# Four dense feed-forward blocks by one level of Strassen's method, gate and up rounds ahead of the down rounds

## The reference, cut to what matters

```python
def _swiglu(h, w_gate, w_up, w_down):
    return (jax.nn.silu(h @ w_gate) * (h @ w_up)) @ w_down
```

## Time and profile before

| | us |
|---|---|
| median of 3 runs | 3219.03 |
| lowest, highest run | 3212.87, 3219.28 |
| span of the profiled execution | 3210.8 |
| PE busy in it | 3114.5 (97%) |
| DVE, ACT busy in it | 798.5 (25%), 487.2 (15%) |
| mean DMA rate over it | 197 GB/s |

### The profile page before, as it was taken

One profiled execution on the slowest core, in us unless ns is written; L12 is line 12 of the kernel. 1 busy time (PEld: TensorE's weight loads), 2 busy tenths in 40 slices (PEclk: granted clock), 3 DMA queues, 4 the chain that ended last, 5 costly groups with the idle time before them and its releaser, 6 DMA issues.

```text
span 3210.8 us, 40563 instructions
## 1 busy us (share of the span) xinstructions
PE 3114.5 (97%) x17087; PEld 2209.2 (69%) x17087; DVE 798.5 (25%) x1696; ACT 487.2 (15%) x1124; POOL 109.5 (3%) x122
## 2 busy tenths in 40 slices
PE   7999998999999999999998999998999999999998
PEld 3566666477777777677776677786777667767765
DVE  2566666410100233300355300132000000100101
ACT  2423332010000123200221200121000000000001
POOL 1121121000000000000000000000000000000000
PEclk8999999999999999999998999999999999999999
DMA  7333127254444522344310345433999999999997
GB/s 249 112 113 124 48 77 292 104 195 155 157 155 147 166 74 81 105 156 147 124 55 16 106 157 166 135 79 125 381 379 382 345 379 382 330 378 382 332 377 259
DMA packets 417831, 636.36 MB, mean 198 GB/s; under 512 B 11247, under 2 KB 304726, under 8 KB 410366
## 3 DMA queue, kind: packets, MB, share of 16 engines
q1 hardware_dynamic: 412317, 612.49, 55.4%
q0 software_dynamic: 5344, 21.46, 2.0%
HBM read 632.70 MB, written 1.20 MB: 197 GB/s over the span
## 4 chain that ended last, share of the span: by engine, by line
PE 89%; DVE 3%; SPq 2%; DMA 1%; ACT 1%; issue 1%; DVEq 1%; PEld 1%; PEldq 0%; ACTq 0%
PE PS L930 18%; PE PS L3830 11%; PE PS L938 7%; PE PS L1399 7%; PE PS L3851 6%; PE PS L3837 6%; PE PS L3877 3%; PE PS L705 2%; PE PS L1975 2%; PE PS L996 2%; PE PS L3324 2%; PE PS L1971 1%; PE PS L1549 1%; PE PS L288 1%; PE PS L1564 1%
## 5 line engine op out<-in xcount | busy, mean ns | idle before, releaser
L957 DVE TENSOR_TENSOR scratch<-scratch,PS 128x128 f32<-128x128 f32 (+1 forms) x182 | 61.7, 339 | 1278.8 <-ACT scratch L947 1278.4
L930 PE MATMUL PS<-XT,WO 128*128 128x256 f32 x1344 | 296.2, 379 | 0.1
L930 PE MATMUL PS<-XT,WF 128*128 128x256 f32 x1344 | 294.7, 379 | 0.0
L930 PEld LDWEIGHTS PS<-XT,WO 128*128 128x128 f32 x1344 | 255.2, 190 | 50.5 <-issue 17.7
L930 PEld LDWEIGHTS PS<-XT,WF 128*128 128x128 f32 x1344 | 255.3, 190 | 46.2 <-issue 12.9
L947 ACT ACTIVATE scratch<-PS 128x128 f32<-128x128 f32 (+1 forms) x200 | 64.9, 324 | 1413.9 <-PE PS L930 776.5
L1399 PE MATMUL PS<-XT,WH 128*128 128x512 f32 x512 | 240.9, 596 | 1.7 <-ACT XT L480 1.7
L3830 PEld LDWEIGHTS PS<-scratch,WO 128*128 128x128 f32 x1792 | 208.6, 192 | 24.9 <-issue 24.6
L3830 PEld LDWEIGHTS PS<-scratch,WF 128*128 128x128 f32 x1792 | 202.4, 192 | 21.3 <-issue 17.9
L3830 PE MATMUL PS<-scratch,WO 128*128 128x128 f32 x1792 | 209.1, 275 | 0.0
L3830 PE MATMUL PS<-scratch,WF 128*128 128x128 f32 x1792 | 207.2, 276 | 1.2 <-ACT scratch L3988 1.2
(11 more groups left out here) (578 smaller groups left out, 3782.6 us busy)
## 6 DMA issues: line engine op xcount, KB each, us to landing
XT<-in_moe_wg SPq DMA_DIRECT2D x56, 1024.0 KB, 10.9
scratch<-in_moe_wu SPq DMA_DIRECT2D x56, 1024.0 KB, 14.1
OT<-in_moe_wd SPq DMA_DIRECT2D x56, 1024.0 KB, 14.1
WO<-in_ada_w SPq DMA_DIRECT2D x36, 1024.0 KB, 7.2
WF<-in_moe_wg SPq DMA_DIRECT2D x28, 1024.0 KB, 15.2
WF<-in_moe_wu SPq DMA_DIRECT2D x28, 1024.0 KB, 17.1
WF<-in_moe_wd SPq DMA_DIRECT2D x28, 1024.0 KB, 12.0
WO<-in_moe_wg SPq DMA_DIRECT2D x28, 1024.0 KB, 11.2
```

What stands on the lines that cost most here:

```text
L930: mm = nc.tensor.matmul(k.PS[:, 4 + f, w * n:(w + 1) * n], slot.gu[:, w, kb, f * P:(f + 1) * P], rhs(kb), start=kb == 0, stop=kb == KB - 1)
```

## The change

Each product of a dense block is cut into 2 x 2 blocks and made from seven block products in place of eight. For a gate and up round the blocks are two tiles of 128 tokens (`t`), two halves of the features (`kh`) and two chunks of 128 hidden units (`fh`); a block product has 8 matmuls of 128 moving columns (gate and up, 4 feature chunks). For a down round they are two token tiles, two hidden chunks and two halves of the 1024 columns; a block product is one matmul of 512 columns. Four of the seven need differences of weight blocks, four need sums of token (or hidden) blocks, which DVE makes ahead; for round 0 of blocks 2 and 3 POOL makes the weight terms. Afterwards DVE puts the seven products together: in every gate and up round (`up_sums_vector`), but only once for the down rounds, since each of their seven products adds up over all rounds in a bank of its own.

All gate and up rounds of a block come first; the hidden units of all rounds stay in SBUF (`hall`); then come all down rounds. At the end, products 7 and 4 of the last 3 rounds (blocks 0, 1) or 6 rounds (blocks 2, 3) are put last (`KEPT`), so that the first token tile is complete earlier. The loops are written out. Raw gate and up weights go to WF and to a piece of scratch, their terms to OT and WO.

```diff
@@ tensor @@
+def up_product(k, m, r, i):
+    weights, tokens = up_sides(k, m, r, i)
+    out = up_place(k, m, r, i)
+    for w in range(2):
+        for kb in range(4):
+            mm = k.nc.tensor.matmul(out[:, w, :], weights[:, w, kb, :], tokens[:, kb, :], start=kb == 0, stop=kb == 3)
+    return mm
+
+def up_first_tensor(k, pe, m, r):
+    pe.wait_ge(*up_landed(k, m, r))
+    up_product(k, m, r, 1)
+    up_product(k, m, r, 2).then_inc(*k.up_pe[r % 2].done("a"))
+
+def up_rest_tensor(k, pe, m, r):
+    S = k.up_pe[r % 2]
+    pe.wait_ge(*terms_at(k, m, r))
+    for i in (4, 6):
+        up_product(k, m, r, i)
+    up_product(k, m, r, 7).then_inc(*S.done("d"))
+    up_product(k, m, r, 5).then_inc(*S.done("e"))
+
+def up_tensor(k, pe, m, r):
+    pe.wait_ge(*sum_at(k, m, r - 2, "sum"))
+    up_first_tensor(k, pe, m, r)
+    up_product(k, m, r, 3).then_inc(*k.up_pe[r % 2].done("raw"))
+    up_rest_tensor(k, pe, m, r)
...
+def ffn_tensor(k, pe, m, flip=None):
...
+    for r in range(2, UP_ROUNDS):
+        up_tensor(k, pe, m, r)
...
+    defer = UP_ROUNDS - KEPT[m]
+    pe.wait_ge(*sum_at(k, m, LAST_UP - 1, "sum"))
+    for q in range(3):
+        down_first_tensor(k, pe, m, q)
+    pe.wait_ge(*sum_at(k, m, LAST_UP, "sum"))
+    for q in range(3):
+        down_next_tensor(k, pe, m, q, (6, 5, 3, 7, 4)).then_inc(*k.dnt_pe.done("t"))
...
+    for q in range(3, UP_ROUNDS):
+        mm = down_first_tensor(k, pe, m, q)
...
+    for i in (7, 4):
+        for q in range(defer, UP_ROUNDS):
+            mm = down_product(k, m, q, i)
+        mm.then_inc(*k.fe_pe.done(f"p{i}"))
@@ vector @@
+def weight_terms(eng, t, block):
+    tt = eng.tensor_tensor
+    tt(t[0], block(0, 1), block(0, 0), ALU.subtract)
+    tt(t[2], block(1, 1), block(0, 1), ALU.subtract)
+    eng.drain()
+    tt(t[1], block(1, 1), t[0], ALU.subtract)
+    eng.drain()
+    return tt(t[3], t[1], block(1, 0), ALU.subtract)
...
+def up_sums_vector(k, dve, m, r):
...
+    dve.wait_ge(*up_copied(k, m, r, "p1"))
+    tt(c(0, 0), k.fp1, place(2), ALU.add)
+    dve.wait_ge(*up_at(k, m, r, "d"))
+    tt(k.fu2, k.fp1, place(6), ALU.add)
+    dve.drain()
+    tt(k.fu3, k.fu2, place(7), ALU.add)
+    dve.drain()
+    tt(c(1, 0), k.fu3, place(4), ALU.subtract)
+    dve.wait_ge(*up_at(k, m, r, "e"))
+    tt(c(0, 1), k.fu2, place(5), ALU.add)
+    tt(c(1, 1), k.fu3, place(5), ALU.add)
+    dve.drain()
+    tt(c(0, 1), c(0, 1), place(3), ALU.add).then_inc(*k.sum_dve[r % 2].done("sum"))
...
+def ffn_vector(k, dve, m, between={}, late=None):
+    for r in range(UP_ROUNDS):
+        up_sums_vector(k, dve, m, r)
+        if r + 2 < UP_ROUNDS:
+            up_terms_vector(k, dve, m, r + 2)
+        else:
+            down_terms_vector(k, dve, m, r + 2 - UP_ROUNDS)
+        hidden_vector(k, dve, m, r)
+        if r in between:
+            between[r]()
+    for q in range(2):
+        hidden_sums_vector(k, dve, m, q)
+    for q in range(2, UP_ROUNDS):
+        down_terms_vector(k, dve, m, q)
+        hidden_sums_vector(k, dve, m, q)
@@ sync @@
+def up_load(k, sp, m, r, weights, *free):
...
+    if r >= 2:
+        sp.wait_ge(*up_at(k, m, r - 2, "raw"))
+        sp.wait_ge(*terms_at(k, m, r - 2))
...
+def down_load(k, sp, m, q, weights, *free):
...
+    if q >= 3:
+        sp.wait_ge(*k.dnr_pe.at("raw", LAST_UP * m + q - 3))
@@ tensor_program @@
-    ffn_tensor(k, pe, 0, 2, lambda: flipped(0, 1, False, k.lno_dve.at("out", 9)), 2)
+    ffn_tensor(k, pe, 2, lambda: flipped(0, 1, False, k.lno_dve.at("out", 9)))
     flipped(1, 0, True, k.dg_dve.at("d", 0))
...
-    ffn_tensor(k, pe, 0, 3, lambda: flipped(2, 1, True, k.dg_dve.at("d", 3)), 1)
+    ffn_tensor(k, pe, 3, lambda: flipped(2, 1, True, k.dg_dve.at("d", 3)))
```

More of the change, by code:

```diff
@@ L138, in done, with __init__, at, both @@
         return self.sem, 1
+class Renamed:
+    def __init__(self, steps, names, past=0):
+        self.steps, self.names, self.past = steps, dict(zip(names.split(), steps.names, strict=True)), past
+    def at(self, name, rnd=0):
+        return self.steps.at(self.names[name], self.past + rnd)
+    def done(self, name):
+        return self.steps.done(self.names[name])
+    def both(self, first, second):
+        return self.steps.both(self.names[first], self.names[second])
 class Kern:
@@ new lines, in down_landed, with ffn_sync @@
+def down_landed(k, m, q):
+    return k.down_in[q % 2], 16 * (half_count(m, q) + 1)
+def ffn_sync(k, sp, m, weights, downs):
+    for r in range(2, LAST_UP - 1):
+        up_load(k, sp, m, r, weights)
+    for q in range(2):
+        before = [k.dnr_pe.at("raw", LAST_UP * (m - 1) + 9), k.fe_pe.at("p3", m - 1)][q:q + 1] if m == 1 else downs
+        down_load(k, sp, m, q, weights, *before)
+    for r in range(LAST_UP - 1, UP_ROUNDS):
+        up_load(k, sp, m, r, weights)
+    down_load(k, sp, m, 2, weights, up_at(k, m, LAST_UP - 1, "e"))
+    for q in range(3, UP_ROUNDS):
+        down_load(k, sp, m, q, weights)
@@ new lines, in down_bank, with down_first_tensor, down_next_tensor @@
+def down_bank(m, i):
+    return DOWN_BANKS[i] ^ (4 * FIRST_SET[m])
+def down_first_tensor(k, pe, m, q):
+    pe.wait_ge(*down_landed(k, m, q))
+    pe.wait_ge(*sum_at(k, m, q, "h"))
+    down_product(k, m, q, 1)
+    return down_product(k, m, q, 2)
+def down_next_tensor(k, pe, m, q, order):
+    pe.wait_ge(*k.dn_dve.at("s", up_count(m, q)))
+    for i in order:
+        mm = down_product(k, m, q, i)
+        if i == 3 and q < LAST_UP:
+            mm.then_inc(*k.dnr_pe.done("raw"))
+        elif i in (5, 6, 3) and q == LAST_UP:
+            mm.then_inc(*k.fe_pe.done(f"p{i}"))
+    return mm
@@ L1098, in end_by_tile_vector @@
[L1098 to L1108 removed]
+    act.wait_ge(*k.fe_pe.at("p12", m))
@@ new lines, in first_tile_vector @@
+def first_tile_vector(k, dve, m):
+    tt, bank = k.nc.vector.tensor_tensor, lambda i: k.PS[:, down_bank(m, i), :]
+    left, right = view(k, 0, 512), view(k, 512, 512)
+    dve.wait_ge(*k.fe_act.at("p1", m))
+    dve.wait_ge(*k.fe_pe.at("p6", m))
+    tt(k.du2, left, bank(6), ALU.add)
+    tt(left, left, bank(2), ALU.add)
+    dve.drain()
+    dve.wait_ge(*k.fe_pe.at("p5", m))
+    tt(right, k.du2, bank(5), ALU.add)
+    dve.drain()
+    dve.wait_ge(*k.fe_pe.at("p3", m))
+    tt(right, right, bank(3), ALU.add).then_inc(*k.lne_dve.done("evac0"))
@@ new lines, in second_tile_vector @@
+def second_tile_vector(k, dve, m, begin=True, end=True):
+    tt, bank = k.nc.vector.tensor_tensor, lambda i: k.PS[:, down_bank(m, i), :]
+    left, right = view(k, D, 512), view(k, D + 512, 512)
+    if begin:
+        dve.wait_ge(*k.fe_pe.at("p7", m))
+        tt(left, k.du2, bank(7), ALU.add)
+        dve.drain()
+        tt(right, left, bank(5), ALU.add)
+    if end:
+        dve.wait_ge(*k.fe_pe.at("p4", m))
+        tt(left, left, bank(4), ALU.subtract).then_inc(*k.lne_dve.done("evac1"))
```

541 lines of the change are left out of this document (323 added, 218 removed).

## The result

The changed kernel takes 3128.5 us (median; 3127.0 to 3129.7), the kernel before 3218.1: a ratio of 0.972, with an interval from 0.971 to 0.974. It saves 89.6 us. Forecast were 3124 us and a saving of 94.7.

The account below looks back on a forecast made before the run. PE was taken to bound the kernel in the four dense blocks. Gains of 104.0 us less losses of 9.3 gave 94.7, so 3219.0 - 94.7 = 3124 us, with a range of 3110 to 3135 (chance 0.70).

Parts of the forecast that it names:

- Gate and up on PE: In the dense blocks a gate and up round of 112 records takes 12.50 us, 1.32 less than before.
- The rival of a slower stream: Gate and up records of 128 columns run slower than the 111.6 ns taken: 3132 to 3149 us; chance 0.07.
- weight loads that show: Loads of 190 to 192 ns do not hide behind 128 columns: 396 us lost, 3520 us; chance 0.02.
- Down on PE: A down round has 14 records in place of 16: 6.01 us, 0.86 less.
- DVE: DVE's work is 9.0 of PE's 12.5 us in gate and up rounds, 4.2 of 6.0 in down rounds; cost 0.
- Its rival: DVE becomes the bound: whole gain gone at 14.7 us a round, about 3366 us at 18; chance 0.03.
- The step: From up to down in each block PE waits 1.2 us for DVE, four times: 4.8 us lost.
- Loads: Gate and up weights land 7.8 us after issue; cost 0, with 2.9 us of slack in the tightest place.
- Clearing and transposes: Bank clearing goes, 1.0 us a block with what surrounds it; transposes of blocks 0 and 1 save 2.6.
- Starts and ends: Starts lose 0 in blocks 0 and 1, 1.6 us in 3; ends lose 0.9, 1.3, 0.7 in 1, 2, 3.
- The first rival: The seams cost some 5 us more in each block: 3144 us, between 3135 and 3160; chance 0.14.
- I take that as unchanged: The runs' median stays 8.2 us above the profiled span after the change, as before it.

Follow-up runs that it names:

- dve4: The changed kernel with four more operations of 1024 elements on DVE ahead of each round's weight terms: 3220.1 us, 91.6 more.
- seam: The changed kernel, with DVE making the last hidden product and down round 0's sums before round 1's weight terms: 3122.2 us, 6.3 less.
- starts: The changed kernel, in blocks 2 and 3 with tile 1's transposes between PE's first products of rounds 0 and 1: 3124.3 us, 4.2 less.
- plain_both: The changed kernel's order of phases with eight plain block products everywhere, no terms or sums: 3216.7 us, ratio 1.0001 to the kernel before.
- after_again: The changed kernel unchanged, measured and profiled once more: 3127.5 us.

## Why the prediction was right, step by step

**The bound.** Right. PE ends the chain before and after, and records taken away were time saved: 52.6 and 61.8 us for the gate and up products (with Strassen's down rounds and with plain ones), 26.4 and 35.6 for the down products. Within the four blocks, without what differs elsewhere, it is 52.4 and 57.3, and 32.3 and 37.1.

**Gate and up on PE.** 12.50 us a round forecast, 12.51 measured; 16 records in 1.79 us are 112 ns each in the rounds behind a block's start. The rival of a slower stream is out, and so is that of weight loads that show. The ratio of 0.62 that the Trainium skill gives for 128 against 512 columns (TensorE: Matmul & The Clock Gate, Back-to-back issue gap) does not hold in this stream; in the changed kernel it is 112 to 429 ns, 0.26 again.

**Down on PE.** 6.01 forecast and found; the last rounds at 4.3 on PE ran without a wait, so the 5 us kept as an upper bound were not needed.

**DVE.** Forecast 9.0 of 12.5 us, busy for 8.2. Its rival was put at 14.7 us a round for the loss of the whole gain; at 13.66 (dve4) the gain was already gone. The sum behind that number counted only the steady rounds. It left out the rounds that also hold the end of a norm, and the slow records that follow a long wait. The conclusion for this kernel stood, but the margin was not one number: DVE's own work is 13.66 less four operations of 1.3, some 8.5 us, which leaves 4 us in a plain round and only 0.4 in a round with a norm's end of 3.6.

**The step.** Forecast 1.2 each; PE idle 0.94, and 1.1 to 1.2 with the stream that starts anew. seam shows that it was DVE's order and that 4.9 us could be had.

**Loads.** Forecast at no cost, with 2.9 us of slack at the tightest place, and PE did not wait for a load in either profile of the changed kernel. The slack was smaller: the weights of round 2 in block 2 were put at 7.8 us to landing and took 8.4 and 9.8, which left 1.8 and 0.4. seam and starts, where they took 10.6 and 11.6, waited for them.

**Clearing and transposes.** Forecast 6.6 gained in all. plain_both has this part without the products, and with it the waits at the starts and ends that the prediction put at 4.5 (0.9 + 1.3 + 1.6 + 0.7). It gains 4.0 in blocks 0 and 1 and loses 1.3 in blocks 2 and 3, 2.8 in all where the terms say 2.1. The size is about right, and it is small next to the products.

**Starts and ends.** Blocks 0, 1 and 3 came out at 25.1, 24.2 and 21.8 us less, against 25.1, 24.2 and 22.2 from the terms. Block 3 has a wait of 0.39 for DVE's sums of token blocks (L1238) that was not foreseen; two of these took 2.14 and 1.37 in place of 0.69, beside a copy on POOL. Block 2 was to give 23.2 and gave 21.2. POOL's terms were put at 10.2 us and took 13.4 there, and 9.7 in block 3, where no DVE operation with two inputs in SBUF ran beside them. Rows of block 2, and two of block 3:

```profile
1281.72 1.23 DVE L743 TENSOR_TENSOR scratch<-PS,WH 128x1024 f32<-128x1024 f32 x1 [5.37 <-PEq L683]
1281.94 2.35 POOL L1246 TENSOR_TENSOR OT<-WF 128x1024 f32<-128x1024 f32 x1 [210.57 <-PEq L683]
1283.03 2.34 DVE L757 SCALAR_TENSOR_TENSOR scratch<-X,scratch 128x1024 f32<-128x1024 f32 x1
1284.26 3.33 POOL L1247 TENSOR_TENSOR OT<-WF 128x1024 f32<-128x1024 f32 x1
...
1289.90 3.22 DVE L780 TENSOR_TENSOR X<-scratch,WH 128x1024 f32<-128x1024 f32 x1
...
1750.81 2.35 POOL L1247 TENSOR_TENSOR OT<-WF 128x1024 f32<-128x1024 f32 x1
1751.33 1.90 DVE L816 TENSOR_SCALAR scratch<-mats,small 128x128 f32<-128x128 f32 x1 [1.85 <-ACT small L237]
```

This is the timeline of the kernel after; in the kernel before, the DVE operations that are L757 and L780 here took 1.23 each. The two engines hold each other up. Of the 13.4 us the four operations are 11.4, and POOL was idle for 1.9 before the third, for which the trace shows no releaser. It cost nothing here, since the terms were there at 1295.3 and PE came to them at 1299.2; but in starts the 2.31 us that PE waits for L780 are mostly the 2.0 that this operation takes longer. In block 3 it is DVE's diagonal (L816, 0.29 elsewhere) that took 1.90 and ended as POOL's L1247 did, at 1753.2; in starts this is the wait of 0.97 at 1753.42. Most of the 2 us of block 2 are in its first 32 records: 6.53 us from start to start where they had taken 3.57, less the 1.7 of slow records that the kernel before had a little later. By after_again, whose block 2 lasts 213.70, 0.8 of them was chance.

**The net.** The terms said 94.7; the blocks gave 92.3, and the two spans differ by 85.7. The first rival, 5 us more for each block, did not come. The larger miss was not in the list of terms: the sum assumed that what lies outside the blocks keeps its time ("What follows the blocks moves as a whole"). The start-up took 1.0 more, the records behind block 2's longer end wait 1.4, the stretch from there to block 3 another 2.1, the router 2.3. The other step that did not hold is "I take that as unchanged": the median lay 8.2 above the profiled span before and 3.4 after. The profiled execution of the kernel before (3212.9) was among its fastest (of 19 others three were below 3214), and its second profile, with a span 4.5 longer, has the slow records that the first lacks. The two errors have opposite signs, 9.0 and 4.8 us, and leave 3128.5 for 3124; that the forecast is only 4.5 off is in part luck. Part of the 9 us is chance in the one profile on which the sum was built. What stays is the end of block 2, slow in both profiles of the changed kernel. The stretch from there to block 3 took 248.5 us in both of them, 245.0 and 246.8 in those of the kernel before, 245.8 to 248.7 in the other ten. Windows about 60 us into it, in the kernel before, in its second profile, and in the kernel after (columns as for dve4's window):

```profile
1625.00:1640.00 15.00, 11.55 (x112) 1.00 0.00 1
...
1626.00:1641.00 15.00, 12.66 (x109) 0.89 0.00 1
...
1556.00:1571.00 15.00, 12.66 (x107) 0.89 0.00 0
```

The clock fell there in every profile but the first of the kernel before, which gains 1.5 us by that. With the 1.4 us of the transposes this is 2.9 of the 3.5 us; the remaining 0.6 is slow records further on. So against the second profile of the kernel before the stretch is 1.8 us longer, and 1.4 of these are the transposes behind the longer wait, the one part that goes with the change. Why the clock falls at the other places in one execution and not in another was not settled.

One slip of the prediction changes nothing: the 9.04 us that it names for rows 10 stand in the earlier trace rows.

## What to carry to other kernels

On a kernel that PE bounds, price a change by records times the pitch of a row with the same shape, engine state and load pattern; that gave 12.50 for 12.51 us, while an assumed eighth of saving would have been a third too much. Work that moves to another engine is free up to the length of the shortest round it shares, so look for the rounds that hold something else too, not for the mean. And at each hand-over between phases write down both chains from the same instant: the one that is longer can often be shortened by doing first what the other engine needs first, as seam did for 5 us with a change of order.
